# Three of six modulation vectors on the matrix engine as rows, four tiles side by side in column groups

## What is computed

```python
silu_c = jax.nn.silu(c)                                   # (1, 2048)
sh1, sc1, g1, sh2, sc2, g2 = jnp.split((silu_c @ w_mod[i] + b_mod[i])[:, None, :], N_MOD, axis=-1)
h_lat = modulate(rms_norm(x, norm_g[i, 0]), sh1, sc1)     # h * (1 + scale) + shift
y_lat = fourier_mix(h_lat) @ fnet_w_out[slot]
x = x + g1 * rms_norm(y_lat, norm_g[i, 1])
x = x + g2 * rms_norm(sqrelu_mlp(modulate(rms_norm(x, norm_g[i, 2]), sh2, sc2), w_mlp_in[i], w_mlp_out[i]), norm_g[i, 3])
```

## Time and profile before

| | |
|---|---|
| median of 3 runs | 2289.96 us (2283.52 to 2290.27) |
| the profiled execution: its own time | 2286.12 us |
| its span (first to last instruction) | 2284.5 us |
| PE busy, share of the span | 2199.5 us, 96% |
| DVE busy | 1370.7 us, 60% |
| ACT busy | 968.1 us, 42% |
| mean granted TensorE clock | 0.968 |
| HBM read | 472.50 MB |

### The profile page before, as it was taken

The page is one execution under the profiler, slowest core; times in us unless marked ns, Lnnn a source line. Parts: engine busy times, 40 slices in busy tenths (PEclk is TensorE's granted clock), DMA queues, the critical chain, the costliest instruction groups (busy, mean ns, idle before and its releaser), DMA issues.

```text
span 2284.5 us, 31892 instructions
## 1 busy us (share of the span) xinstructions
PE 2199.5 (96%) x11881; PEld 1897.3 (83%) x11881; DVE 1370.7 (60%) x1323; ACT 968.1 (42%) x1126; POOL 47.4 (2%) x68
## 2 busy tenths in 40 slices
PE   6888999999999999999899999998999999999999
PEld 6876789888888888887888879887888888888887
DVE  5779877655655655566567545654654654555553
ACT  3132334443444444343543347744443443444342
POOL 0000010000000000001000000000000000000000
PEclk8899987999999999999899989999999999999999
DMA  9888988667666767767465535664666666666664
GB/s 370 314 310 285 357 303 288 207 219 220 202 220 209 214 208 218 215 207 228 138 172 145 146 93 146 191 193 134 184 193 192 184 192 190 186 188 192 187 187 156
DMA packets 219174, 478.77 MB, mean 210 GB/s; under 512 B 14708, under 2 KB 15084, under 8 KB 218336
## 3 DMA queue, kind: packets, MB, share of 16 engines
q1 hardware_dynamic: 211940, 450.98, 62.2%
q0 software_dynamic: 6192, 24.64, 3.5%
q10 hardware_dynamic: 972, 2.19, 0.3%
HBM read 472.50 MB, written 5.24 MB: 209 GB/s over the span
## 4 chain that ended last, share of the span: by engine, by line
PE 86%; DVE 5%; DMA 5%; ACT 2%; issue 2%; SPq 0%; DVEq 0%; ACTq 0%
PE ps L390 21%; PE ps L408 13%; PE ps L410 13%; PE ps L409 13%; PE ps L391 11%; PE ps L394 3%; PE ps L396 3%; PE ps L395 3%; DVE acc L1098 1%; DMA raw<-in_w_mod_dram 1%; PE ps L432 1%; DMA raw<-in_w_mem_kv_dram 1%; PE ps L451 1%; DMA raw<-in_w_in_dram 1%; DVE wl L1073 1%
## 5 line engine op out<-in xcount | busy, mean ns | idle before, releaser
L1073 DVE TENSOR_TENSOR wl<-raw,wh 128x1024 fp32r<-128x1024 f32 x688 | 813.2, 1222 | 358.8 <-ACT wh L774 357.6
L774 ACT ACTIVATE wh<-raw 128x1024 fp32r<-128x1024 f32 x688 | 701.3, 1053 | 616.2 <-DMA raw<-in_w_down_dram 163.8
L390 PE MATMUL ps<-xt,wh 128*128 128x512 f32 x2048 | 725.0, 399 | 0.0
L391 PE MATMUL ps<-xt,wl 128*128 128x256 f32 x2048 | 575.4, 281 | 0.0
L390 PEld LDWEIGHTS ps<-xt,wh 128*128 128x128 f32 x2048 | 386.1, 189 | 95.5
L408 PE MATMUL ps<-wh,u 128*128 128x512 f32 x1152 | 449.0, 390 | 0.0
L409 PE MATMUL ps<-wl,u 128*128 128x512 f32 x1152 | 448.2, 389 | 0.0
L410 PE MATMUL ps<-wh,u 128*128 128x512 f32 x1152 | 448.1, 389 | 0.0
L391 PEld LDWEIGHTS ps<-xt,wl 128*128 128x128 f32 x2048 | 387.9, 189 | 0.2
L408 PEld LDWEIGHTS ps<-wh,u 128*128 128x128 f32 x1152 | 216.2, 188 | 45.5 <-issue 0.5
L410 PEld LDWEIGHTS ps<-wh,u 128*128 128x128 f32 x1152 | 216.2, 188 | 45.0
(11 more groups left out here) (251 smaller groups left out, 1621.8 us busy)
## 6 DMA issues: line engine op xcount, KB each, us to landing
raw<-in_w_mod_dram SPq DMA_DIRECT2D x160, 512.0 KB, 6.2
raw<-in_w_mlp_in_dram SPq DMA_DIRECT2D x128, 512.0 KB, 3.8
raw<-in_w_mlp_out_dram SPq DMA_DIRECT2D x128, 512.0 KB, 4.3
raw<-in_w_up_dram SPq DMA_DIRECT2D x128, 512.0 KB, 3.7
raw<-in_w_down_dram SPq DMA_DIRECT2D x128, 512.0 KB, 4.2
raw<-in_w_in_dram SPq DMA_DIRECT2D x96, 512.0 KB, 3.7
raw<-in_fnet_w_out_dram SPq DMA_DIRECT2D x32, 512.0 KB, 5.2
slot<-in_w_mod_dram POOLq DMA_DIRECT2D x32, 512.0 KB, 4.6
```

The costliest lines, as they stand in the source:

```text
L390: mm(o, a, flat(xt[:, kt, :, :]), start=first, stop=end, skip_group_check=True)
L391: last = mm(o[:, 0:S], b, xt[:, kt, 0, :], start=False, stop=end, skip_group_check=True)
L774: A(flat(wh[:, i, :, :]), raw[:, landed[0], :], ACT.Copy).then_inc(sem("w_hi"), 1)
L1073: V.tensor_tensor(flat(wl[:, s, :, :]), raw[:, s, :], flat(wh[:, i, :, :]).bitcast(F32), ALU.subtract).then_inc(sem("w_lo"), 1)
```

## The change

sc1 and sh2 go to PE whole, and half of sh1 (16 tiles in four runs of four). `mod_chunk` is replaced by `mod_rows`: silu(c) of one block, copied 32 times (`silu32`, one DVE copy at the start), is the stationary operand (128 rows x 32 columns), and the tile itself is the moving one, in two pieces of 512 columns. Four tiles go to the four groups of 32 columns of the matrix engine (`tile_position`), so that each writes 32 partitions of a PSUM bank. A quad (four tiles) is 8 products, 16 passes, and frees its four ring slots when it is done. Once for each half DVE adds the rows to the accumulator (`fold`, scaled by 1/32), and `mod_sum` runs as before, now 8 or 16 products that begin their own sums. All six vectors' tiles now come in the order half 0, half 1. The sum of sc1 moves behind the third chunk of `w_mem_kv`; the transposes of `h` move behind the third quad (`SH2_TURN`); on DVE two MLP remainders move ahead of the last fold.

```diff
+PE_MOD = dict(sc1=range(0, 32), sh1=(0, 1, 2, 3, 8, 9, 10, 11, 16, 17, 18, 19, 24, 25, 26, 27), g1=(), sc2=(), sh2=range(0, 32))
+QUAD = 4
...
         tmp = at("tmp", [P, 4, S], F32, O_TMP)
         slot = at("slot", [P, MODC], F32, O_SLOT)
...
 
...
 
-        def mod_part(vec, n):
-
-            return (n % KT, n // KT) if vec == "sh2" else divmod(n, 2)
+        def mod_part(n):
+
...
+            def mod_rows(vec, c0, n0, bank):
+
+                mine = [n for n in PE_MOD[vec] if n // KT == n0 // KT]
+                tiles = [(n % KT, mod_c(c0, n)) for n in range(n0, n0 + QUAD)]
+                for _, cc in tiles:
+                    s, r = slot_of(cc)
+                    pe.wait_ge(sem(f"raw_landed{s}"), 16 * r)
+                for col in range(2):
+                    for j, (kt, cc) in enumerate(tiles):
+                        last = mm(ps[j * QP:(j + 1) * QP, bank + col, :], silu32[:, kt, :],
+                                  raw[:, cc % RAW, col * GC:(col + 1) * GC], start=n0 == mine[0], stop=n0 + QUAD - 1 == mine[-1],
+                                  skip_group_check=True, tile_position=(0, j * QP))
+                        if col == 1:
+                            last.then_inc(mod_used(cc)[0], 1)
+
+            def mod_sum(a, bank, halves=(0, 1)):
+
                 for kt in range(8 * halves[0], 8 * halves[-1] + 8):
-                    last = mm(ps[:, bank, kt:kt + 1], (acc[0], acc[1], acc2)[a][:, kt * P:(kt + 1) * P], ones[:, 0:1], start=alone, stop=True,
+                    last = mm(ps[:, bank, kt:kt + 1], (acc[0], acc[1], acc2)[a][:, kt * P:(kt + 1) * P], ones[:, 0:1], start=True, stop=True,
                               skip_group_check=True)
                 last.then_inc(sem("mod_mm"), 1)
 
...
-
-            pe.wait_ge(sem("silu_ready"), 1)
-            for n in range(MODN):
-                if n in (4, 6, 8, 10):
-                    transposes(0, y, [(n - 4) // 2])
-                if n in PE_MOD["sc1"]:
-                    mod_chunk("sc1", C_SC1, n, 2, n == PE_MOD["sc1"][0])
+            pe.wait_ge(sem("silu_ready"), 2)
+            for n in range(0, MODN, QUAD):
+                mod_rows("sc1", C_SC1, n, 2 * (n // KT))
+                if n == 0:
+                    transposes(0, y, [0, 1])
+                if n in (4, 8):
+                    transposes(0, y, [1 + n // 4])
             pe.wait_ge(sem("const_set"), 2)
-            mod_sum("sc1", C_SC1, 0, 2)
-
-            def sh1_chunks(m):
-                for n in (2 * m, 2 * m + 1):
-                    if n in PE_MOD["sh1"]:
-                        mod_chunk("sh1", C_MEM, n, 7, n == PE_MOD["sh1"][0])
+            pe.wait_ge(sem("rows_folded"), 1)
+
+            def sh1_rows(m):
+                if 2 * m + 1 in PE_MOD["sh1"][3::4]:
+                    if m >= CH:
+                        pe.wait_ge(sem("rows_folded"), 3)
+                    mod_rows("sh1", C_MEM, 2 * m - 2, 6)
 
             for i in range(CH):
                 if i % 2 == 0:
                     pe.wait_ge(sem("xt_ready"), 1 + i // 2)
                 T_chunk(G_MEM, i, False, *early(i))
-                sh1_chunks(i)
+                sh1_rows(i)
+                if i == 2:
+                    pe.wait_ge(sem("rows_folded"), 2)
...
+                    mod_sum(0, 2)
-                sh1_chunks(CH + i)
+                sh1_rows(CH + i)
...
-            mod_sum("sh1", C_MEM, 1, 7)
+            pe.wait_ge(sem("rows_folded"), 4)
+            mod_sum(1, 7)
...
             pe.wait_ge(sem("slot_used"), 2)
-            mod_sum("sc2", C_FN, 1, 7)
-            pe.wait_ge(sem("evacuated"), G_ML1 - 1)
-            for n in range(MODN):
-                if n == KT:
-                    mod_sum("sh2", C_SH2, 2, 0, (0,))
+            for n in (KT - 1, MODN - 1):
+                pe.wait_ge(*mod_used(mod_c(C_FN, n)))
+            mod_sum(1, 7)
+            for n in range(0, MODN, QUAD):
+                if n == 0:
+                    pe.wait_ge(sem("evacuated"), G_ML1 - 1)
                 if n == SH2_TURN:
                     pe.wait_ge(sem("mod_out"), 3)
                     transposes(1, h, drained="x1t_out")
                     pe.wait_ge(sem("x1t_out"), 4)
-                if n in PE_MOD["sh2"]:
-                    mod_chunk("sh2", C_SH2, n, 7 * (n // KT), n in (PE_MOD["sh2"][0], min(m for m in PE_MOD["sh2"] if m >= KT)))
-            mod_sum("sh2", C_SH2, 2, 7, (1,))
+                if n == KT:
+                    pe.wait_ge(sem("evacuated"), G_ML1)
+                mod_rows("sh2", C_SH2, n, 2 * (n // KT))
+                if n == KT:
+                    pe.wait_ge(sem("rows_folded"), 5)
+                    mod_sum(2, 6, (0,))
+            pe.wait_ge(sem("rows_folded"), 6)
+            mod_sum(2, 7, (1,))
...
-                kt, half = mod_part(vec, n)
+                kt, half = mod_part(n)
...
+            def fold(vec, c0, half, a, bank):
+
+                dve.wait_ge(*mod_used(mod_c(c0, [n for n in PE_MOD[vec] if n // KT == half][-1])))
+                if (vec, half) in summed:
+                    dve.wait_ge(*summed[vec, half])
+                t = (acc[0], acc[1], acc2)[a][:, half * MODC:(half + 1) * MODC].rearrange("p (b n) -> p b n", b=2)
+                V.scalar_tensor_tensor(out=t, in0=ps[:, bank:bank + 2, :], scalar=1.0 / QP, in1=t,
+                                       op0=ALU.mult, op1=ALU.add).then_inc(sem("rows_folded"), 1)
...
+            V.tensor_copy(silu32[:, :, :], siluc[:, :].rearrange("p (k o) -> p k o", o=1).to_broadcast([P, KT, QP])).then_inc(sem("silu_ready"), 1)
...
-                gemv("sc1", C_SC1, n, 0)
+                if n == KT:
+                    dve.wait_ge(sem("acc0_seeded"), 16)
+                    fold("sc1", C_SC1, 0, 0, 0)
+            fold("sc1", C_SC1, 1, 0, 2)
             dve.wait_ge(sem("acc1_seeded"), 16)
             for m in range(2 * CH):
                 lo_static(m)
                 for j in range(2):
                     gemv("sh1", C_MEM, 2 * m + j, 1)
-                if m == 2:
+                if m % CH == CH - 1:
+                    fold("sh1", C_MEM, m // CH, 1, 6)
+                if m == 4:
                     mod_vector(1, vtmp[:, :], 2)
                     link(V.tensor_scalar(vtmp[:, :], vtmp[:, :], 1.0, None, ALU.add))
                     link(V.tensor_tensor(a1[:, :], v("ng0", KT), vtmp[:, :], ALU.mult))
...
-            for n in range(MODN):
-                if n == 1:
-                    y_block(GQ - 1)
-                    mean(4, 3, "sq", 12)
-                    dve.wait_ge(sem("evacuated"), G_ML1)
-                    for piece in range(4):
-                        residual(piece)
-                if n == 3:
-                    mod_vector(3, vtmp[:, :], 7)
-                    link(V.tensor_scalar(vtmp[:, :], vtmp[:, :], 1.0, None, ALU.add))
-                    V.tensor_tensor(a2[:, :], v("ng2", KT), vtmp[:, :], ALU.mult).then_inc(sem("a2_ready"), 1)
-                if n == 4:
-                    mean(2, 4, "hsq", 4)
-                    diagonals()
-                if n == 18:
-                    shift_half(0)
-                if n in (21, 26):
-                    shifted_lo((n - 21) // 5)
-                gemv("sh2", C_SH2, n, 2)
-            lo_static(CH * G_ML1)
+            y_block(GQ - 1)
+            mean(4, 3, "sq", 12)
+            dve.wait_ge(sem("evacuated"), G_ML1)
+            for piece in range(4):
+                residual(piece)
+            mod_vector(3, vtmp[:, :], 7)
+            link(V.tensor_scalar(vtmp[:, :], vtmp[:, :], 1.0, None, ALU.add))
+            V.tensor_tensor(a2[:, :], v("ng2", KT), vtmp[:, :], ALU.mult).then_inc(sem("a2_ready"), 1)
+            mean(2, 4, "hsq", 4)
+            diagonals()
+            fold("sh2", C_SH2, 0, 2, 0)
+            shift_half(0)
+            for r in range(2):
+                shifted_lo(r)
+            for r in range(2):
+                lo_static(CH * G_ML1 + r)
+            fold("sh2", C_SH2, 1, 2, 2)
             shift_half(1)
-            lo_static(CH * G_ML1 + 1)
             for r in (2, 3):
                 shifted_lo(r)
                 lo_static(CH * G_ML1 + r)
...
-SH2_TURN = 6
+SH2_TURN = 12
```

More of the change, by code:

```diff
@@ L47 @@
 MODN = KT * D // MODC
-PE_MOD = dict(sc1=(2, 5, 8, 11, 13, 16, 18, 21, 24, 27), sh1=(3, 7, 11, 15, 19, 23), sc2=(), sh2=(3, 5, 8, 11, 14, 17, 20, 23, 25, 28))
+PE_MOD = dict(sc1=range(0, 32), sh1=(0, 1, 2, 3, 8, 9, 10, 11, 16, 17, 18, 19, 24, 25, 26, 27), g1=(), sc2=(), sh2=range(0, 32))
+QUAD = 4
+QP = P // QUAD
 EPS = 1e-6
@@ L102, in program @@
         slot = at("slot", [P, MODC], F32, O_SLOT)
+        silu32 = at("silu32", [P, KT, QP], F32, 64 * KB)
         xn = at("xn", [P, 2, HALVES, D], F32R, O_U)
@@ L194, in slot_of @@
             return cc % RAW, cc // RAW + 1
-        def mod_part(vec, n):
-            return (n % KT, n // KT) if vec == "sh2" else divmod(n, 2)
+        def mod_part(n):
+            return n % KT, n // KT
         def mod_c(c0, n):
@@ L265, in _ @@
```

(10 more changed lines are left out.)

2 lines of the change are left out of this document (removed).

## The result

The changed kernel takes 2298.8 us (median of 5; 2297.07 to 2304.11), the kernel before 2288.4 beside it on the same chip: ratio 1.0057, 95% interval 1.0039 to 1.0075. That is slower, by 10 us; 2297 had been forecast. The executions of one kernel, taken side by side, lie within 12 us of each other but for one: of the last experiment's six, one took 10,734 us, which its ratio leaves out and its median of 2279.44 does not (2278.82 without it).

What follows compares the result with a forecast made beforehand. The front was taken as bound by when ring slots come free, and by DVE in the Fourier stage. Terms +4.4 - 2.6 + 3.0 + 2.0 = +6.8 on 2289.96 gave 2297 us, range 2283 to 2318.

Steps and rivals of the forecast that it cites:

- the likeliest case: Whole kernel: the summed terms give +6.8 us, 2297 us, own range 2289 to 2303; chance 0.60.
- its main sign: No sign is called main; first listed: Fourier stage, four `gemv` in 5.45 us instead of 4.87, steps 7.96 apart.
- The quad's price: 16 passes on PE in four column groups, taken as four deep: 1.8 us warm, 3.6 cold.
- Both rivals that rested on fewer groups at once: Column groups only two deep: 2317 us, chance 0.13; no overlap at all: about 2361 us, chance 0.07.
- g1, +4.4: Fourier stage: four `gemv` in a row become dependent, steps go from 7.39 to 7.96 us, DVE has no slack: +4.4.
- The head, -2.6: Behind sc1: PE starts T at 67.5 instead of 71.95, -4.4; the first sh1 quad holds four slots 1.8 more: -2.6.
- sh1's other quads, +3.0: Three later sh1 quads leave holes of 2.5 us each, mostly absorbed by 4.7 us already lost: +3.0, bounds 0 and 7.5.
- sc1, "worth nothing": sc1 stage: 22 `gemv` and 10 `mod_chunk` go, but the loads set that stage anyway, so no gain.
- The stage of sh2, +2.0: sh2 up to the first MLP product: last tile lands 2.6 us earlier, longer tail: +2.0, bounds -3 and +6.
- The tail of 9.5 us: Last sh2 tile's landing to first MLP product: 10.1 us cold, 8.3 warm, 9.5 used, instead of 4.9 before.
- The rival in which the gaps close: PE stays warm, the 62 to 82 gap closes, sh1 costs 0, sh2 gains 3: -5.6, 2284 us; chance 0.20.

Runs made afterwards that it cites:

- the last experiment: Changed kernel with pairs, g1 alternating, last sh2 fold ahead of the MLP remainders, and GpSimd's memset of y behind the diagonals of h: 2279.44 us, 0.9966.
- pairs: Changed kernel with two tiles per PE group instead of four, each tile's column halves in two column groups, in sc1, sh1 and sh2: 2285.96 us, 0.9995.
- the repeat: The changed kernel run once more, unedited: 2299.91 us, 1.005 times the kernel before.

## Why the prediction was right, and where not

The forecast of 2297 and the measured 2298.8 agree, the likeliest case came, and its main sign too. That the two lie so close is in part luck: the forecast stood on 2289.96 for the kernel before, which measured 2288.4 and 2286.93 in the two comparisons, and the sum came to +6.8 where 10 to 13 were measured (12.4 and 15.0 at M). Of the terms g1 was sized well and sh2 lay in its bounds; the head and sh1 failed in their mechanism.

- **The quad's price** (1.8 warm, 3.6 cold): 1.92 and 3.3 to 3.64. Right, from a row on row groups that only lay near it. The estimate by the Trainium skill (page "TensorE: Matmul & The Clock Gate", section "Part 3: Packing small matmuls") was 3.1; the trace doesn't agree, with four groups where the page has three. Both rivals that rested on fewer groups at once fall with it.
- **g1, +4.4**: +4.5 and +4.3 from F to S, and gone when g1 alternates (146.6 against 145.98 before). Right, mechanism and size; DVE has no slack there.
- **The head, -2.6**: +0.3 at the same load issue (76.98, now 77.27). This step failed: "The first sh1 quad, behind the second chunk, holds four slots for 1.8 more". It holds them through the second chunk's products as well, since PE goes in order: the products of the first two chunks run from 67.93 to 75.40 and the quad to 77.25. With -4.0 for the earlier start, 1.92 for the quad and some 3 for that chunk's products the term would have come to +1.
- **sh1's other quads, +3.0**: the holes were sized rightly (landing gaps of 4.1, 3.7 and 4.2 us where a load needs 1.3, so 2.8, 2.4 and 2.9 against the 2.5 worked out). What failed is "most of these fall into the new holes". From load 41 to load 79 the changed kernel lost 7.5 us, nearly the 8.1 of the holes; the 4.7 us that the stage wasted before were no stock to pay from. That the holes are the cause is not shown by this sum: without any sh1 quad the same stretch lost 7.9. The first of these holes also left PE idle for 3.42 us, and the chunk behind it ran cold (5.5 us from 103.94, where warm ones take 3.1).
- **sc1, "worth nothing"**: near for quads, by a wrong reason. The last sc1 tile (load 31) lands at 61.63 in the changed kernel, 62.84 before: the 374 GB/s are not sc1's tiles coming later, but the loads behind them being issued later (load 32 at 60.33 instead of 56.57). What failed is the sentence that the loads set that stage. A share of 1.00 at 387 GB/s looked like the ceiling; with pairs it was 408, and load 31 landed at 58.80. What sc1's quads cost comes behind the last tile, as the kernel with sh1 and the sum as before showed (T 3.0 late, load 79 at 145.5).
- **The stage of sh2, +2.0**: +3.6 and +1.5 in two executions, inside its bounds. The tail of 9.5 us was 9.8 and 11.1, and 6.5 with the fold moved.
- **The rival in which the gaps close** did not come: quads hold slots. The pairs came near it, at 2285.96 or 0.9995 times the kernel before (2288.11 beside it), where that rival had 5.6 us less than before.

Of the 13.5 us at load 79 between quads and pairs, 8.0 are thus shown to be the wait for four tiles (with sh1's other places), in which tiles stand in their slots until three more have landed; the other 5.5 come with the layout, and why is open. How much of the 6.4 us against the kernel before is due to either depends on what is undone first: the pairs' layout with the quads' waits was only 0.9 late (140.1). How the loss splits between sc1 and sh1 is open too. Taking the quads out of sh1 alone gave 0.7 us at load 79, and 7.2 where the sum stood first, so the three edits ahead of F don't add. And 3 of the 6.3 us by which sh1 and the sum as before stay late have no row that I could name.

## What to carry to other kernels

An instruction that takes n slots of a ring at once is to be priced by the slots: each is held from its own landing until the last one has landed, the engine has come round in its order, and the work is done; spread one tile over more of the engine before putting more tiles side by side. A DMA share near 1.00 doesn't prove that the loads are the bound, as it was read ahead of the experiments: the same stage moved 374, 387, 394 and 408 GB/s at shares of 0.97 to 1.03, and what differed was by whom and when the slots were freed. And an edit that merely changes the order of accumulation can turn independent neighbours into dependent ones: here that alone was 4.5 of the 15 us at the first MLP product (4.3 of 12.4 in the repeat).

## What the runs showed of the hardware beside that

Four column groups of 32 run side by side almost fully: 16 passes of 512 float32 columns in 1.92 us against 7.05 in one group, and 8 passes of two tiles, each with its halves in two groups, in 1.06.

A small DVE operation was stretched by a memset on GpSimd. Timelines of POOL and DVE in the changed kernel, then of DVE in the one with the memset behind the diagonals:

```profile
329.38 3.51 POOL L338 MEMSET y<- 128x4096 f32 x1 [4.25 <-DVE h L1279]
```

```profile
329.43 3.48 DVE L1306 TENSOR_SCALAR vtmp<-vtmp 128x16 f32<-128x16 f32 x1
```

```profile
314.06 0.17 DVE L1308 TENSOR_SCALAR vtmp<-vtmp 128x16 f32<-128x16 f32 x1
```

The addition on 16 columns ends as the memset ends, and takes 0.17 us without it (3.48 in the same kernel with the memset beside it). In the kernel before the same addition took 0.90 us: it starts at 320.62, and the memset ends at 321.49. A copy and a product on 128x16 right before and after it took 0.17 each.
